# A convolution tile as three rounded products, and another pace for taps and norms in a two-block transformer kernel

## The chip, the core and the metric

The kernel runs on one core of a Trainium2 chip. The metric is the device time of one execution in microseconds; it is the time of the whole program, two layers of a first kind of block and then two layers of a second. Engines: PE (TensorE) multiplies matrices, DVE (VectorE), ACT (ScalarE) and POOL (GpSimd) work on tiles of 128 partitions, SP issues the weight DMAs. Each engine runs its own instructions in the order in which they are written, and waits on semaphores that the others raise.

## The reference, cut

Sequence 512, width 1024, float32. The change lies in the mixer of the first kind of block, which does attention with a window and a causal depthwise convolution of 31 taps side by side on one projection:

```python
u = _rms_norm(h, mix_norm[i])
q, k, v, ca, cg = jnp.split(u @ w_in[i], SPLITS, axis=-1)
q = _partial_rope(q.reshape(B, S, N_HEADS, HEAD_DIM), positions)
k = _partial_rope(k.reshape(B, S, N_KV_HEADS, HEAD_DIM), positions)
attn = _sliding_window_attention(q, k, v, sinks[i])
conv = _conformer_conv(ca, cg, conv_w[i], conv_b[i], conv_ln_g[i], conv_ln_b[i])
mixed = jnp.concatenate([_rms_norm(attn, attn_out_norm[i]),
                         _rms_norm(conv, conv_out_norm[i])], axis=-1)
h = h + mixed @ w_out[i]
...
def _conformer_conv(a, g, w_dw, b_dw, ln_g, ln_b):
    u = a * jax.nn.sigmoid(g)
    y = conv(u, w_dw) + b_dw        # 512 channels, each with 31 taps over time
    return jax.nn.silu(_layer_norm(y, ln_g, ln_b))
```

Around it stand two gated FFNs of 2816, a projection of a per-layer embedding (`p[i] @ w_ple[i]`, normed, "the embedding" below) and a gate. The second kind of block is not touched.

## The kernel before

**Layout and precision.** Activations lie transposed, features on partitions and 512 time steps along the free axis, in tiles of 128x512. A weight product in near full precision is three products of rounded operands (type fp32r): ACT rounds a 128x1024 weight tile (`act_split`, L328, raw to wh), DVE takes the remainder (`dve_split`, L332, wl), and PE does hi x hi, hi-weight x lo, lo-weight x hi (L346 to L348, or `pe_chunks`, L356 to L358). A "unit" is one such output tile: 8 chunks of 128 rows, 24 products. Weights stream by DMA from SP through four buffers. PE may start unit k when wl of k is there and the bank of unit k-2 has been read.

**The stage of the change** (`block1`) has three parts.

*Projections*, 14 units n = 0 to 13: convolution gate and value (n 0 to 7), keys (8), values (9), queries (10 to 13). In each, DVE reads the bank (L1106), takes the next weight remainder, multiplies gate and value into `upad` (odd n), later rotates keys and queries (`rotate`, L1061 to L1072) and does `TAPS_AFTER[n]` taps of the second channel tile (L1081, L1085, a running sum in PSUM). ACT rounds weights, does three tap products a unit (`act_tap`, L877 and L883, for channel tiles 0 and 2) and builds 31 diagonal matrices `diag` of the fourth tile's taps (L887). POOL adds ACT's products (L675); ACT may be three products ahead.

*Pairs*, m = 0 to 15, four heads' pairs for each of four query blocks. PE runs scores (L758, two pairs ahead), turn (L770, transposes of the probabilities) and values (L783); DVE `scale` (L1143) takes the scores and their maximum, ACT `exps` (L945) the exponentials, DVE `turn_back` (L1154) copies the turned probabilities. Between them stand: the 31 taps of the fourth channel tile on PE (L791, a diagonal matrix times a shifted input, in full float32), the rest of ACT's taps (five a pair) and DVE's, the layer norm's mean (L831, pair 6) and variance (L837, pair 8), its root on ACT (L965) and reciprocal and products on DVE (L1223, L1226, pair 10), the SiLU on ACT (L969, pair 11), eight embedding tiles on PE (L745 to L747, pairs 7 to 14) that DVE copies (L1130) and ACT squares (L931), and the output norm's statistic (L843, pair 13). `pe_fill` (L420) issues products whose result nobody reads: 4 at pair 5, 4 at pair 11, 6 behind the pairs.

*Tail*: attention norm (L1179) and output norm of the convolution (L1234, L1237), transposes of the attention output (L797), the embedding's statistic (L851), rounding to `fh` and `fl` (L983, L1242, L990, L1185), and the first two units of the output projection, whose convolution chunks (4 to 7) come before their attention chunks (0 to 3).

The order is written out by hand in the five engine functions.

## Time and profile before

| | us |
|---|---|
| median of 3 runs | 3876.05 |
| lowest, highest | 3874.99, 3879.52 |
| the profiled execution | 3877.19 |
| its span in the trace | 3875.4 |
| PE busy in the span | 3761.7 |
| DVE, ACT, POOL busy | 2353.7, 1511.6, 532.9 |
| mean granted clock of PE | 0.993 |

The profiled execution is a run of its own, so its time is not one of the three. Times in the timelines count from the start of the span. A count of PE rows counts records: a product in full float32 leaves two. "[1.90 <-ACT prob L945]" says that the engine stood idle for 1.90 us and that an instruction of ACT that wrote `prob` released it. A PE record lasts longer than its share of the array, since products overlap: the pace is the distance between starts. The granted clock is 1.00 at 2.4 GHz and 0.50 at 1.2 GHz.

### The profile page before, as it was taken

The numbers are of one execution on the slowest core, as the hardware profiler recorded it, in microseconds if no ns is written. First come the engines' busy times: TensorE is split into PE (matmuls) and PEld (weight loads), VectorE is DVE, ScalarE is ACT, GpSimd is POOL, SyncE is SP. The second block draws the span as 40 slices with busy tenths as digits, with TensorE's granted clock in tenths as the row PEclk, the third lists the DMA queues.
The fourth block names the chain that finished last, engine by engine and source line by source line (L and its number), as shares of the span: only waits on it lengthen the run. The fifth ranks groups of instructions, "written<-read, shape, count | busy, mean of one in ns | idle before, by whom it ended". The sixth has DMA issues, their size and how long they took to land.

```text
span 3875.4 us, 46681 instructions
## 1 busy us (share of the span) xinstructions
PE 3761.7 (97%) x17846; PEld 3061.1 (79%) x17846; DVE 2353.7 (61%) x3233; ACT 1511.6 (39%) x2191; POOL 532.9 (14%) x378
## 2 busy tenths in 40 slices
PE   8999989999999999999999999999999999999997
PEld 6888758888888885788887778788877878888886
DVE  5455766444644467744567685675568776675656
ACT  3223653222422265422243554343344454343333
POOL 1001641000100046100010023200010013220002
PEclk9999999999999999999999999999999999999999
DMA  4333203333333330233333100132233210023222
GB/s 151 97 98 105 81 17 93 98 98 100 105 97 95 97 109 22 68 98 98 97 107 103 56 28 1 39 98 94 97 105 120 66 39 7 12 87 98 95 96 82
DMA packets 87019, 315.01 MB, mean 81 GB/s; under 512 B 10016, under 2 KB 10400, under 8 KB 86176
## 3 DMA queue, kind: packets, MB, share of 16 engines
q1 hardware_dynamic: 83664, 302.43, 25.2%
q10 hardware_dynamic: 3152, 9.74, 0.8%
q8 instruction: 143, 2.34, 0.3%
q14 instruction: 60, 0.49, 0.0%
HBM read 307.94 MB, written 2.10 MB: 80 GB/s over the span
## 4 chain that ended last, share of the span: by engine, by line
PE 84%; DVE 10%; POOL 2%; ACT 2%; issue 2%; DMA 0%; DVEq 0%; POOLq 0%; ACTq 0%; SPq 0%
PE ps L346 20%; PE ps L348 20%; PE ps L347 20%; PE ps L356 4%; PE ps L358 3%; PE ps L357 3%; POOL y L675 1%; PE ps L2021 1%; DVE wl L332 1%; PE ps L1690 1%; PE ps L2040 1%; PE ps L1682 1%; PE ps L1847 1%; POOL rstd L390 1%; DVE tri L1657 1%
## 5 line engine op out<-in xcount | busy, mean ns | idle before, releaser
L328 ACT ACTIVATE wh<-raw 128x1024 fp32r<-128x1024 f32 x564 | 597.4, 1059 | 1595.1 <-PE ps L348 1312.4
L346 PE MATMUL ps<-xh,wh 128*128 128x512 f32 x2336 | 917.3, 393 | 11.5 <-DVE xl L411 10.9
L347 PE MATMUL ps<-xl,wh 128*128 128x512 f32 x2336 | 910.0, 390 | 0.0
L348 PE MATMUL ps<-xh,wl 128*128 128x512 f32 x2336 | 909.8, 389 | 0.0
L332 DVE TENSOR_TENSOR wl<-raw,wh 128x1024 fp32r<-128x1024 f32 x564 | 704.7, 1249 | 176.2 <-ACT wh L328 175.2
L346 PEld LDWEIGHTS ps<-xh,wh 128*128 128x128 f32 x2336 | 439.3, 188 | 107.9 <-issue 12.5
L347 PEld LDWEIGHTS ps<-xl,wh 128*128 128x128 f32 x2336 | 439.4, 188 | 93.9 <-issue 3.6
L348 PEld LDWEIGHTS ps<-xh,wl 128*128 128x128 f32 x2336 | 439.3, 188 | 91.7
L346 PE MATMUL ps<-fh,wh 128*128 128x512 f32 x1016 | 397.3, 391 | 4.0 <-DVE wl L332 4.0
L347 PE MATMUL ps<-fl,wh 128*128 128x512 f32 x1016 | 395.4, 389 | 0.0
L348 PE MATMUL ps<-fh,wl 128*128 128x512 f32 x1016 | 395.3, 389 | 0.0
L390 POOL TENSOR_TENSOR rstd<-rstd,sq 128x512 f32<-128x512 f32 x77 | 124.3, 1614 | 1649.8 <-ACT sq L385 1648.9
L508 DVE SCALAR_TENSOR_TENSOR h<-ps,h 128x512 f32<-128x512 f32 x144 | 99.5, 691 | 316.6 <-PE ps L348 245.2
L346 PEld LDWEIGHTS ps<-fh,wh 128*128 128x128 f32 x1016 | 190.7, 188 | 48.2 <-DVE wl L332 8.5
L348 PEld LDWEIGHTS ps<-fh,wl 128*128 128x128 f32 x1016 | 190.7, 188 | 39.7
L347 PEld LDWEIGHTS ps<-fl,wh 128*128 128x128 f32 x1016 | 190.7, 188 | 39.6 <-issue 0.5
L576 DVE TENSOR_TENSOR ubuf<-ps,rstd 128x512 f32<-128x512 f32 x88 | 60.8, 691 | 263.2 <-PE ps L348 263.2
L356 PE MATMUL ps<-xh,wh 128*128 128x512 f32 x448 | 194.8, 435 | 5.9 <-DVE wl L332 3.9
L675 POOL TENSOR_TENSOR y<-y,tap_out 128x512 f32<-128x512 f32 x120 | 171.7, 1431 | 81.2 <-ACT tap_out L883 73.7
L573 DVE TENSOR_TENSOR gbuf<-ps,rstd 128x512 f32<-128x512 f32 x88 | 60.8, 691 | 192.6 <-PE ps L348 192.5
L358 PE MATMUL ps<-xh,wl 128*128 128x512 f32 x448 | 176.3, 393 | 0.0
L357 PE MATMUL ps<-xl,wh 128*128 128x512 f32 x448 | 175.5, 392 | 0.0
(477 smaller groups left out, 5575.2 us busy)
## 6 DMA issues: line engine op xcount, KB each, us to landing
raw<-in_w SPq DMA_DIRECT2D x564, 512.0 KB, 3.5
con<-in_consts SPq DMA_DIRECT2D x1, 2053.5 KB, 14.1
h<-in_x SPq DMA_DIRECT2D x4, 512.0 KB, 7.1
p_t<-in_p ACTq DMA_DIRECT2D x4, 512.0 KB, 3.8
w1k<-in_w1c ACTq DMA_DIRECT2D x2, 1024.0 KB, 5.3
w1v<-in_w1c ACTq DMA_DIRECT2D x2, 1024.0 KB, 7.4
out<-h SPq DMA_DIRECT2D x8, 256.0 KB, 2.1
dup_k<-roped ACTq DMA_DIRECT2D x8, 128.0 KB, 3.5
```

The costliest lines, as they stand in the source:

```text
L328: nc.scalar.activation(wh[k % 2][:, :], raw[k % 4][:, :], ACT.Copy).then_inc(s["w_hi"], 1)
L332: nc.vector.tensor_tensor(wl[k % 2][:, :], raw[k % 4][:, :], wh[k % 2][:, :].bitcast(F32), ALU.subtract).then_inc(s["w_lo"], 1)
L346: nc.tensor.matmul(DB[k % 2][:, :], a, hi(q), start=(q == order[0]), stop=False)
L347: nc.tensor.matmul(DB[k % 2][:, :], a, lo(q), start=False, stop=False)
L348: last = nc.tensor.matmul(DB[k % 2][:, :], b, hi(q), start=False, stop=(q == order[-1]))
L356: nc.tensor.matmul(DB[k % 2][:, :], a, hi(q), start=start and n == 0, stop=False)
L357: nc.tensor.matmul(DB[k % 2][:, :], a, lo(q), start=False, stop=False)
L358: last = nc.tensor.matmul(DB[k % 2][:, :], b, hi(q), start=False, stop=stop and n == len(chunks) - 1)
L390: nc.gpsimd.tensor_tensor(acc[:, :], acc[:, :], sq[:, n % 2, :], ALU.add).then_inc(s["sq_add"], 1)
L508: nc.vector.scalar_tensor_tensor(h[:, j, :], DB[k % 2][:, :], factor, h[:, j, :], ALU.mult, ALU.add).then_inc(s["bank"], 1)
L573: v.tensor_tensor(gbuf[:, :], DB[k % 2][:, :], rstd[:, :], ALU.mult).then_inc(s["bank"], 1)
L675: nc.gpsimd.tensor_tensor(y[:, ct, :], y[:, ct, :], tap_out[:, i % 3, :], ALU.add)\
```

## The change

Four edits, all in `block1`, so twice in the program.

1. The fourth channel tile's 31 taps on PE are each three fp32r products: `diag_hi` x `up_hi`, `diag_hi` x `up_lo`, `diag_lo` x `up_hi`. ACT rounds the tile's taps (`tap_hi`) and its input (`up_hi`, 128x542); DVE takes both remainders and builds 31 matrices `diag_lo`. PE waits for `up_lo` before the first tap.
2. ACT's tap products: 45 in the projections and 4 behind them, then four a pair, instead of 36 and five a pair. DVE's taps of the second tile: four a pair instead of three.
3. Norms sooner: mean at pair 5, variance at 7, root and reciprocal at 8, SiLU at 9, embedding tiles at pairs 6 to 13, output statistic at 11, its root at 12 and its reciprocal at 13. Attention norms of three blocks and the second output weight's split at pair 14, and the roundings of the convolution in ACT's pair 14.
4. The fills are gone, and the tail's order on PE is: transposes of three blocks, last values, convolution chunks of unit 1, the embedding's statistic, half of the chunks of unit 0, last transposes, the other half, attention chunks.

```diff
+            PLE_AT = 6
+            SILU_AT = 9
+            TAPS_UNDER = (0, 0, 4, 3, 4, 3, 4, 3, 4, 4, 4, 4, 4, 4)
+            TAPS_AHEAD = 4
...
                     def tap(j):
                         pe.wait_ge(s["diag"], z("diag") + j + 1)
-                        mm(BK[4][:, :], diag[:, j, :], upad[:, PE_CT, j:j + T], start=(j == 0),
+                        mm(BK[4][:, :], diag_hi[:, j, :], up_hi[:, j:j + T], start=(j == 0), stop=False)
+                        mm(BK[4][:, :], diag_hi[:, j, :], up_lo[:, j:j + T], start=False, stop=False)
+                        mm(BK[4][:, :], diag_lo[:, j, :], up_hi[:, j:j + T], start=False,
                            stop=(j == TAPS - 1)).then_inc(s["tap"], 1)
...
-                        if m == 5:
-                            pe_fill(DB[0], 4)
                         turn(m)
...
-                        if m == 11:
-                            pe.wait_ge(s["o_ready"], z("o_ready") + 2)
-                            pe_fill(DB[0], 4)
...
-                    pe_fill(BK[2], 6)
...
+                    for i in range(done, done + TAPS_AHEAD):
+                        act_tap(act, s, st, i)
+                        done += 1
...
-                        for _ in range(5):
+                        for _ in range(4):
                             if done < N_PROD:
                                 act_tap(act, s, st, done)
...
+                        if m == 14:
+                            act_split(act, s, st, 0, o + U1_OUT + 1)
+                            for q in range(CT):
+                                act.wait_ge(s["conv_normed"], z("conv_normed") + q + 1)
+                                A(fh[:, 4 + q, :], y[:, q, :], ACT.Copy).then_inc(s["conv_hi"], 1)
...
+                        if n < 5:
+                            for j in range(7 * n, min(7 * n + 7, TAPS)):
+                                v.tensor_scalar(diag_lo[:, j, :], c("ident"), tap_lo[:, j:j + 1], None, ALU.mult)
+                        if n == 8:
+                            dve.wait_ge(s["gate"], z("gate") + 6)
+                            v.tensor_tensor(up_lo[:, :], upad[:, PE_CT, :], up_hi[:, :].bitcast(F32),
+                                            ALU.subtract).then_inc(s["conv_in"], 1)
...
+                        if m == 13:
+                            dve.wait_ge(s["cn_root"], z("cn_root") + 1)
+                            v.reciprocal(rstd[:, :], rstd[:, :]).then_inc(s["dve_step"], 1)
+                            dve.wait_ge(s["dve_step"], z("dve_step") + st.up("dve_step"))
+                            for q in range(CT):
+                                v.scalar_tensor_tensor(y[:, q, :], y[:, q, :], g("conv_out")[:, q:q + 1],
+                                                       rstd[:, :], ALU.mult, ALU.mult).then_inc(s["conv_normed"], 1)
+                        if m == 14:
+                            dve_split(dve, s, st, 0, o + U1_OUT + 1)
...
+                            for b in range(NB - 1):
+                                norm_o(b)
```

The order of ACT from the tap products of the last two projection units to those behind pair 1 and the exponentials next to them, before:

```order
L883 ACTIVATE tap_out<-upad,small_73 128x512 x4
L921 ACTIVATE p_hi<-p_t 128x1024
L328 ACTIVATE wh_59<-raw_57 128x1024
L945 ACT_TABLE_LOAD
L945 ACTIVATE prob,den<-sm,negm 128x128 x2
L883 ACTIVATE tap_out<-upad,small_73 128x512 x5
L945 ACTIVATE prob,den<-sm,negm 128x128 x2
L883 ACTIVATE tap_out<-upad,small_73 128x512 x5
L945 ACTIVATE prob,den<-sm,negm 128x128 x2
```

and with the change:

```order
L890 ACTIVATE tap_out<-upad,small_73 128x512 x8
L932 ACTIVATE p_hi<-p_t 128x1024
L328 ACTIVATE wh_59<-raw_57 128x1024
L890 ACTIVATE tap_out<-upad,small_73 128x512 x4
L959 ACT_TABLE_LOAD
L959 ACTIVATE prob,den<-sm,negm 128x128 x2
L890 ACTIVATE tap_out<-upad,small_73 128x512 x4
L959 ACTIVATE prob,den<-sm,negm 128x128 x2
L890 ACTIVATE tap_out<-upad,small_73 128x512 x4
```

The row of eight holds the four products of each of the last two units (before: one of unit 12 and the three of unit 13, the others in rows above). Four more stand behind the weight rounding, ahead of the first exponentials, and then four instead of five in each pair.

DVE in the ninth projection unit (n = 8), before:

```order
L1085 SCALAR_TENSOR_TENSOR ps<-upad,small_73,ps 128x512 x2
L1106 TENSOR_TENSOR gbuf<-ps,rstd 128x512
L332 TENSOR_TENSOR wl_60<-raw_56,wh_58 128x1024
L1085 SCALAR_TENSOR_TENSOR ps<-upad,small_73,ps 128x512 x4
L1106 TENSOR_TENSOR v_t<-ps,rstd 128x512
L332 TENSOR_TENSOR wl_61<-raw_57,wh_59 128x1024
```

and with the change:

```order
L1101 SCALAR_TENSOR_TENSOR ps<-upad,small_73,ps 128x512 x2
L1122 TENSOR_TENSOR gbuf<-ps,rstd 128x512
L332 TENSOR_TENSOR wl_60<-raw_56,wh_58 128x1024
L1141 TENSOR_TENSOR up_lo<-upad,up_hi 128x542
L1101 SCALAR_TENSOR_TENSOR ps<-upad,small_73,ps 128x512 x4
L1122 TENSOR_TENSOR v_t<-ps,rstd 128x512
L332 TENSOR_TENSOR wl_61<-raw_57,wh_59 128x1024
```

The remainder of the inputs stands ahead of the four taps.

DVE from the copy of the embedding in pair 13 (ple 5 of 0 to 7) to the last norm of the attention blocks, before:

```order
L1130 COPY e_t<-ps 128x512
L1154 COPY pt<-ps 128x512
L1130 COPY e_t<-ps 128x512
L1154 COPY pt<-ps 128x512
L1160 TENSOR_TENSOR es<-negm,small_73 128x8
L1130 COPY e_t<-ps 128x512
L1154 COPY pt<-ps 128x512
L1229 RECIPROCAL ss<-ss 128x3
L1179 SCALAR_TENSOR_TENSOR o_tok<-o_tok,ss,small_73 128x512 x3
L1234 RECIPROCAL rstd<-rstd 128x512
L1237 SCALAR_TENSOR_TENSOR y<-y,small_73,rstd 128x512 x4
```

and with the change, from pair 13 too (ple 6), to the turn of pair 15:

```order
L1158 COPY e_t<-ps 128x512
L1182 COPY pt<-ps 128x512
L1258 RECIPROCAL rstd<-rstd 128x512
L1261 SCALAR_TENSOR_TENSOR y<-y,small_73,rstd 128x512 x4
L1158 COPY e_t<-ps 128x512
L1182 COPY pt<-ps 128x512
L1188 TENSOR_TENSOR es<-negm,small_73 128x8
L332 TENSOR_TENSOR wl_61<-raw_55,wh_59 128x1024
L1266 RECIPROCAL ss<-ss 128x3
L1207 SCALAR_TENSOR_TENSOR o_tok<-o_tok,ss,small_73 128x512 x3
L1182 COPY pt<-ps 128x512
```

The reciprocal and the four products of the output norm now stand before the turns of pairs 14 and 15, and with them a weight remainder and three attention norms.

## Rows read from the trace of the kernel before

**Rows 1.** The page, its first part: busy time of each engine, share of the span, instructions.

```profile
PE 3761.7 (97%) x17846; PEld 3061.1 (79%) x17846; DVE 2353.7 (61%) x3233; ACT 1511.6 (39%) x2191; POOL 532.9 (14%) x378
```

**Rows 2.** Timeline of PE, 456 to 520: start, length, engine, line, operands, count, idle time before.

```profile
459.17 0.39 PE L347 MATMUL ps<-xl,wh 128*128 128x512 f32 x1
459.40 0.39 PE L348 MATMUL ps<-xh,wl 128*128 128x512 f32 x1
...
471.62 1.13 PE L758 MATMUL ps<-k_z,q_t 128*128 128x128 f32 x8 [0.56 <-DVE q_t L1072]
...
482.89 4.51 PE L791 MATMUL ps<-upad,diag 128*128 128x512 f32 x10
487.24 1.02 PE L758 MATMUL ps<-k_z,q_t 128*128 128x256 f32 x4
...
500.95 0.66 PE L770 MATMUL ps<-con,prob 128*128 128x128 f32 x4 [1.90 <-ACT prob L945]
...
511.47 3.67 PE L831 MATMUL ps<-y,con 128*128 128x512 f32 x8 [0.17 <-issue]
514.98 1.03 PE L758 MATMUL ps<-k_z,q_t 128*128 128x256 f32 x4
515.85 0.60 PE L770 MATMUL ps<-con,prob 128*128 128x128 f32 x4
516.28 1.00 PE L783 MATMUL ps<-v_tok,pt 128*128 128x64 f32 x8
517.09 0.48 PE L745 MATMUL ps<-p_hi,wh 128*128 128x512 f32 x1
```

**Rows 3.** Timeline of PE, 520 to 600, columns as above.

```profile
536.93 3.65 PE L420 MATMUL ps<-con 128*128 128x512 f32 x8
541.87 0.47 PE L745 MATMUL ps<-p_hi,wh 128*128 128x512 f32 x1 [1.28 <-DVE e_t L1130]
...
565.23 5.31 PE L420 MATMUL ps<-con 128*128 128x512 f32 x12
...
585.53 0.41 PE L346 MATMUL ps<-fh,wh 128*128 128x512 f32 x1
```

**Rows 4.** Timeline of POOL, 383 to 620: the additions of convolution taps.

```profile
457.43 8.74 POOL L675 TENSOR_TENSOR y<-y,tap_out 128x512 f32<-128x512 f32 x5 [1.42 <-ACT tap_out L883]
474.48 36.73 POOL L675 TENSOR_TENSOR y<-y,tap_out 128x512 f32<-128x512 f32 x26 [8.31 <-ACT tap_out L883]
```

**Rows 5.** Timeline of DVE, 383 to 600, beside an idle and a busy POOL.

```profile
421.83 1.23 DVE L332 TENSOR_TENSOR wl<-raw,wh 128x1024 fp32r<-128x1024 f32 x1 [0.33 <-ACT wh L328]
...
446.68 2.25 DVE L332 TENSOR_TENSOR wl<-raw,wh 128x1024 fp32r<-128x1024 f32 x1
...
461.61 1.76 DVE L1061 TENSOR_TENSOR fbuf<-gbuf,cos 128x512 f32<-128x512 f32 x1
...
466.36 0.68 DVE L1061 TENSOR_TENSOR fbuf<-ubuf,cos 128x512 f32<-128x512 f32 x1
...
533.60 3.34 DVE L1223 RECIPROCAL rstd<-rstd 128x512 f32<-128x512 f32 x1
536.97 3.34 DVE L1226 TENSOR_TENSOR y<-y,rstd 128x512 f32<-128x512 f32 x4
...
567.12 2.74 DVE L1237 SCALAR_TENSOR_TENSOR y<-y,small,rstd 128x512 f32<-128x512 f32 x4
```

**Rows 6.** Groups of DVE instructions by line: count, busy us and mean ns.

```profile
L550 DVE TENSOR_SCALAR turn<-turn 128x512 f32<-128x512 f32 x4 | 1.7, 429 | 0.1
```

**Rows 7.** Timeline of ACT, 383 to 595: the load of a function table.

```profile
554.40 1.28 ACT L977 ACT_TABLE_LOAD   x1
```

**Rows 8.** Timeline of PE in the second layer, 1498 to 1520.

```profile
1506.31 0.66 PE L770 MATMUL ps<-con,prob 128*128 128x128 f32 x4 [1.89 <-ACT prob L945]
...
1508.48 4.92 PE L420 MATMUL ps<-con 128*128 128x512 f32 x8
```

**Rows 9.** Two us there: length, busy PE, PEld, DVE, ACT, POOL, then PE's granted clock.

```profile
1508.00:1510.00 2.00, 2.00 (x4) 1.01 (x3) 1.93 (x6) 0.87 (x2) 1.84 (x3) 0.50 0.00 0
```

More of the change, by code:

```diff
@@ L845, in _, with conv_chunks @@
                             last.then_inc(s["cn_mm"], 1)
-                    values(PAIRS - 1)
                     for b in range(NB - 1):
                         out_tiles(b)
+                    values(PAIRS - 1)
+                    def conv_chunks(n, chunks):
+                        k = o + U1_OUT + n
+                        pe.wait_ge(s["w_lo"], k + 1)
+                        for q in chunks:
+                            pe.wait_ge(s["conv_lo"], z("conv_lo") + q - 3)
+                            pe_chunks(k, f_hi, f_lo, (q,), q == 4, False)
+                    conv_chunks(1, range(4, DC))
                     pe.wait_ge(s["e_add"], z("e_add") + DC - 1)
@@ L886, in act_diag @@
                 def act_diag(act, s, st, j):
[L887 removed]
+                    nc.scalar.activation(diag_hi[:, j, :], c("ident"), ACT.Copy,
                                          scale=taps[:, PE_CT, j:j + 1]).then_inc(s["diag"], 1)
@@ L907, in _ @@
                     done = built = 0
+                    A(tap_hi[:, :], taps[:, PE_CT, :], ACT.Copy).then_inc(s["gate"], 1)
                     for n in range(14):
@@ L913, in _ @@
                             A(sbuf[:, :], v_t[:, :], ACT.Sigmoid).then_inc(s["gate"], 1)
-                        for i in range(done, done + 3 if n >= 2 else done):
+                        if n == 8:
+                            act.wait_ge(s["conv_in"], z("conv_in") + CT)
+                            A(up_hi[:, :], upad[:, PE_CT, :], ACT.Copy).then_inc(s["gate"], 1)
+                        for i in range(done, done + TAPS_UNDER[n]):
                             act_tap(act, s, st, i)
```

105 lines of the change are left out of this document (50 added, 55 removed).

## The prediction

> **What bounds the kernel now.** I read the page first: PE is busy for 97% of the span [rows 1], so time is to be had only where PE idles, waits behind padding, or does work that could be cheaper. The edits touch one stretch, the mixer of the first block type, which runs twice. In the first layer it runs from the projections (from 384) to 585.5, where the third tile of the output projection starts [rows 3]. The timelines of the four engines over that stretch, in one clock, tell the rest. The reader is to see three parts.
>
> From about 446 to 471.6 PE waits for DVE: PE's scores of pair 0 start at 471.62, after a wait that a DVE instruction writing q_t ended [rows 2]. From 471.6 to 511.5 PE is nearly always busy, but its turn of pair 4 waits 1.90 us for ACT's exponentials [rows 2], and those queue behind ACT's tap products, which wait for POOL: POOL adds 26 taps in one run of 36.73 us, so 1.41 us each, until 511.2 [rows 4]. The mean of the layer norm needs the last of them, and PE starts it at 511.47 [rows 2]. So POOL sets the mean. From there to 585.53 (74.1 us) the chain goes to and fro between PE, DVE and ACT: 14 fill products pad PE's waits in a layer, two groups of 4 and one of 6 [rows 3]. I call the start of the scores S and the start of the mean M; before, M = S + 39.85.
>
> **Step 1, the taps of TensorE.** Five taps in full precision run from 482.89 to 487.24, 0.87 us a tap [rows 2]. The three products that replace each are of the form that the projections use, which start 0.23 us apart [rows 2]: 3 x 0.227 = 0.68 us. That is 0.19 us a tap, 31 taps, 5.9 us a layer, if PE bounds. The first 7 taps lie before S, where PE waits for DVE, and give nothing.
>
> **Step 2, S moves.** ACT now issues 49 tap products ahead of the first exponentials, not 36. POOL therefore has 47 additions, not 34, before S. Its idle gaps from 402 to 466 add up to about 11 us (10 gaps, the last of 1.42 us [rows 4]), and 13 additions of 1.36 us are 17.7 us. So POOL is busy without a break up to S and DVE works beside it. What this does to DVE is in the rows: the weight remainder takes 1.23 us beside an idle POOL and 2.25 beside a busy one; the rotation's product 0.68 against 1.76 [rows 5]. DVE has no slack left from the ninth projection tile on. On its chain to S the change puts:
> - the remainder of the rounded inputs (128x542, two operands from SBUF), 0.7 to 1.8 us; I take 1.3;
> - weight remainders of tiles 7, 8, 9 and 11 that now meet a busy POOL: 0.8 + 0.9 + 0.9 + 0.5 = 3.1 us;
> - the last two rotation products, at 466.4 and 469.3, now beside a busy POOL: 2 x 1.1 us and about 0.3 us on the sums behind them, 2.5 us.
> Together 6.9 us: S at 478.5 and not 471.6. The bounds: 0.7 us, if POOL cost nothing, and about 8.5. The 31 small products that build diag_lo (seven a tile) lie in the first five tiles; a 128x512 of that kind takes 0.43 us [rows 6], so at most 0.25 us each, 1.8 us a tile, about DVE's idle time there. I take nothing for them.
>
> No row shows this one-input operation beside a busy POOL. The Trainium skill, GPSIMD Engine Reference, Key points, says that GpSimd shares its SBUF interfaces with VectorE and that they contend when a VectorE instruction has two SBUF inputs or runs in a 2-port mode. For two inputs the trace agrees (0.68 against 1.76 us). By that rule the small products of tiles 2 to 4 would contend too, and the sum would grow towards rival C's; by the rows alone it stays.
>
> **Step 3, from S to M.** After S, PE's rows give each pair: scores 0.87, turn 0.43, values 0.8 [rows 2] (half of that for the first four pairs, which have one block of keys). Scores 0 and 1: 0.96. Pair 0: 5 taps 3.4 + 0.44 + 0.22 = 4.1. Pair 1: 4.5. Pairs 2 and 3: 4.9 each. Pair 4 with the last 4 taps: 4.45. Then scores, turn and values before the mean, which now stands behind pair 5: 2.2. The sum is 26.0. DVE's reading of the taps' bank, behind the end of the first query block, adds about 0.4. POOL has 13 additions left, 13 x 1.41 = 18.3 us after S, so it no longer sets M; ACT's exponentials, paced by four additions a pair (5.6 us against PE's 4.9), start two pairs ahead: those of pair 3 end at about 495.3, and PE's turn of it is due at 498.9. Against this, PE idles about 3.3 us before the last rotation and 3.8 before S, and the clock falls. Its price is in the second layer: after a wait of 1.89 us the stretch at 1508 shows a clock of 0.50, that is 1.2 and not 2.4 GHz, and eight fill records take 4.92 us [rows 8, 9] and not 3.65 [rows 3]. A longer dense stretch at that level costs somewhat more; I take 1.7. M = 478.5 + 26.4 + 1.7 = 506.6, that is 4.9 us sooner than 511.47.
>
> **Step 4, from M to the end.** I walked the chain with the durations of the rows, M as zero. One more pair stands behind the mean than before (10, not 9): 2.1 us of PE. Up to the variance nothing differs. The first reciprocal (3.34) with its four products (3.34) [rows 5] blocks DVE from 19.2 to 25.8, before PE had 3.65 us of fill and 1.28 of wait there [rows 3], now it waits 5.5. So these 4 fills buy nothing, and nor do the four behind pair 5: a wait takes their place. The output norm's statistics run at 38.2 to 41.7 and its root on ACT ends at 46.7. Each change between exponential and root costs ACT a table load of 1.28 [rows 7]: exponentials of pair 13 end at 49.0, PE turns at 49.2, DVE copies to 50.4, and only then come the second reciprocal and four products (3.34 + 2.74 [rows 5]) to 56.4. **That is the place that decides.** On DVE the last embedding copy, the turn of pair 14, a weight remainder and three attention norms are queued behind them; on ACT the weight rounding and four roundings of the convolution (some 5 us) stand ahead of the exponentials of pair 15, which end at 62.4. PE has nothing else and idles from 55.6 to 62.5. Before, the same norm ended at 58.4, but pairs 14 and 15 were done by then; now it ends at 56.4 with them open. Behind: turn and values 14 to 63.9, three transposes of the output to 65.7, values 15, four chunks (waiting once for DVE) to 70.1, the statistic 71.0, two chunks, transpose, two chunks to 74.3, and the eight attention chunks 5.5: 79.9. Before it was 74.1. So the stretch grows by 5.9 us although 12.2 us of fill left PE. On top the clock falls in the wait of 5.5 and in that of 7 us, both without fill now: 1.6 + 1.9 us.
>
> **The sum.** Per layer -4.9 + 5.9 + 3.5 = +4.5. In the second layer one such fall was there already (4.92 against 3.65), so +3.2. Together **+7.7 us**. The profiled execution took 3877.19 us (span 3875.4); it lies 1.1 us above the median of 3876.05, and I add the sum to the median: 3884 us. Nothing else in the program moves. A measurement of this kernel can tell about 0.2%, 7.75 us, from no change, so the forecast stands on that line.
>
> **Rivals.**
> A, the other side: **POOL does not slow DVE further**, because the additions fall where DVE reads PSUM. Then S = 472.3, M = 472.3 + 26.4 = 498.7, 12.8 us sooner. With the falls of the clock behind M (3.5) a layer gives -12.8 + 5.9 + 3.5 = -3.4, in all about -8: 3868. If the short waits also leave the clock up: -6.9 a layer, -15 in all, 3861. It decides at S: below about 475 the kernel is faster. For it: POOL still has slack in tiles 2 to 7, where fours and threes alternate. Against it: from tile 8 on there are four in every tile, and the rows of a busy POOL.
> B: **the clock does not fall** in the new waits, with S as forecast: -6.6 + 5.9 = -0.7 a layer, 3873, no change. Against it stands the fall after 1.89 us of wait [rows 8]; for it, that a like wait at 500.95 [rows 2] left the 4 fills behind it at 3.65 us.
> C: **the projections themselves stall**: four additions with the locks (1.36 x 4 + 1.6 = 7 us) are more than a tile's 5.44 us, ACT's tap products wait for POOL and the weight rounding behind them on ACT's queue comes late, and the small diagonal products each wait for an addition. Up to 6 us a layer more: 3896.
> D: the second norm's chain is shorter than walked (say the root is ready a pair earlier), 4 us a layer: 3876.
>
> **How the numbers follow.** Forecast 0.38, half of it beyond the line. A 0.22 (0.15 of it faster by over 0.2%), B and D 0.22, C 0.18. That gives faster 0.17, within 0.2% 0.42, slower 0.41. The range must reach to A with the clock kept and to C: 3861 to 3897.
>
> **What the profile would show.** S in the first layer at 478 (less than 474 for A, over 482 for C); the mean at 506; POOL's additions ended before 500; taps in triples 0.68 us apart; a PE wait of over 5 us for the embedding copy behind the reciprocal and one of over 6 before the turn of pair 15; a clock of 0.5 behind each; third tile of the output projection at about 590. The prediction is wrong if S does not move, or if the wait before pair 15 is under 3 us.

## The result and the profile after

The changed kernel takes 3882.59 us (median of 20 runs, 3881.07 to 3885.18), the kernel before 3877.41 us (20 runs beside it, 3874.99 to 3879.52). The ratio is 1.0014, with a 95% interval from 1.0008 to 1.002: 5.2 us slower, 0.14%. The forecast was 7.7 us slower. The profiled execution has a span of 3880.7 us (before 3875.4). Every experiment below is set against runs of the kernel before made beside it, whose medians lie between 3876.0 and 3877.6 us.

I read each trace by four points. All are counted from the first statistic product of the projections (before: 384.80 in the first layer, 1390.19 in the second). S is the start of the scores of pair 0, M that of the mean, T the last turn, E the third tile of the output projection.

| kernel, layer | S | M | T | E | M to E |
|---|---|---|---|---|---|
| before, 1 | 86.82 | 126.67 | 175.00 | 200.73 | 74.1 |
| before, 2 | 86.79 | 126.67 | 175.01 | 202.33 | 75.7 |
| after, 1 | 92.46 | 122.16 | 185.44 | 204.33 | 82.2 |
| after, 2 | 92.40 | 121.37 | 184.37 | 202.79 | 81.4 |

So the mean came 4.5 and 5.3 us sooner, and the stretch behind it grew by 8.1 and 5.8 us: +3.6 and +0.5 us. The rest of the 5.3 us of span lies outside: -0.4 us ahead of the first layer, and behind the second 2282.9 us before and 2284.5 after, where the diff changes nothing. Over all the kernels of this study that last stretch reads 2280.5 to 2285.8 us in the profiled executions, so 1.6 us there is no effect of the change.

TensorE's timeline of the changed kernel, first layer (start, length, engine, line, operands, count, idle time before and what ended it), answers to [rows 2, 3]:

```profile
476.89 2.05 PE L765 MATMUL ps<-k_z,q_t 128*128 128x128 f32 x8 [2.88 <-DVE q_t L1088]
478.59 0.77 PE L798 MATMUL ps<-up_hi,diag_hi 128*128 128x512 f32 x1
479.16 0.63 PE L799 MATMUL ps<-up_lo,diag_hi 128*128 128x512 f32 x1
479.59 0.63 PE L800 MATMUL ps<-up_hi,diag_lo 128*128 128x512 f32 x1
...
484.68 0.48 PE L798 MATMUL ps<-up_hi,diag_hi 128*128 128x512 f32 x1
485.00 0.39 PE L799 MATMUL ps<-up_lo,diag_hi 128*128 128x512 f32 x1
485.23 0.39 PE L800 MATMUL ps<-up_hi,diag_lo 128*128 128x512 f32 x1
...
488.25 0.60 PE L765 MATMUL ps<-k_z,q_t 128*128 128x128 f32 x4
...
506.59 3.67 PE L835 MATMUL ps<-y,con 128*128 128x512 f32 x8 [0.35 <-DVE y L1242]
...
532.98 0.80 PE L752 MATMUL ps<-p_hi,wh 128*128 128x512 f32 x1 [4.27 <-DVE e_t L1158]
...
557.12 0.66 PE L777 MATMUL ps<-con,prob 128*128 128x128 f32 x4 [2.54 <-ACT prob L959]
...
569.87 1.11 PE L777 MATMUL ps<-con,prob 128*128 128x128 f32 x4 [6.10 <-ACT prob L959]
570.78 1.80 PE L790 MATMUL ps<-v_tok,pt 128*128 128x64 f32 x8
...
588.76 0.41 PE L346 MATMUL ps<-fh,wh 128*128 128x512 f32 x1
```

Where fills stood before there are waits of 4.27 and 6.10 us now. Behind the waits of 2.88, 4.27 and 6.10 us the products start at about half their rate: the tap products 0.43 us apart, and 0.23 from 482.9 on. The windows view of these stretches shows the granted clock (the number behind POOL's) at 0.50, that is 1.2 GHz. It shows the same from 558 to 561, behind the wait of 2.54 us:

```profile
478.00:482.00 4.00, 4.00 (x13) 3.32 (x12) 1.26 (x8) 3.97 (x9) 3.78 (x3) 0.50 0.00 0
533.00:534.00 1.00, 1.00 (x3) 0.81 (x4) 0.52 (x1) 0.59 (x1) 0.27 (x1) 0.50 0.00 0
559.00:560.00 1.00, 1.00 (x4) 0.81 (x4) 1.00 (x1) 0.97 (x3) 0.61 (x1) 0.50 0.00 0
570.00:574.00 4.00, 4.00 (x20) 4.00 (x21) 2.67 (x6) 0.53 (x1) 0.00 (x0) 0.50 0.28 103
```

GpSimd's timeline (additions of taps, against [rows 4]) and DVE's (against [rows 5]) of the changed kernel:

```profile
414.14 41.42 POOL L682 TENSOR_TENSOR y<-y,tap_out 128x512 f32<-128x512 f32 x25 [2.90 <-ACT tap_out L890]
455.88 45.66 POOL L682 TENSOR_TENSOR y<-y,tap_out 128x512 f32<-128x512 f32 x29 [0.32 <-ACT tap_out L890]
```

```profile
396.02 1.46 DVE L1138 TENSOR_SCALAR diag_lo<-con,tap_lo 128x128 fp32r<-128x128 f32 x7
...
408.58 3.53 DVE L1138 TENSOR_SCALAR diag_lo<-con,tap_lo 128x128 fp32r<-128x128 f32 x7
...
429.49 1.51 DVE L332 TENSOR_TENSOR wl<-raw,wh 128x1024 fp32r<-128x1024 f32 x1 [2.67 <-ACT wh L328]
...
436.22 1.79 DVE L1141 TENSOR_TENSOR up_lo<-upad,up_hi 128x542 fp32r<-128x542 f32 x1
...
469.95 1.71 DVE L1077 TENSOR_TENSOR fbuf<-ubuf,cos 128x512 f32<-128x512 f32 x1
...
476.66 1.23 DVE L1160 TENSOR_SCALAR negsink<-small 128x8 f32<-128x8 f32 x1
```

From 414 to 501.5 GpSimd works without a break (one gap of 0.32 us). Seven of the small products for diag_lo take 1.46 us while it idles, and 3.53 beside it. The rotation's product that took 0.68 us [rows 5] takes 1.71. An operation on 128x8 takes 1.23 us; its like in the kernel before, at 471.39, took 0.16. From the wait of 2.67 us at 429.49, for ScalarE's rounding of the next weights, DVE has no further idle time up to S.

And the place before the last turn, on DVE, then on ScalarE:

```profile
558.42 3.34 DVE L1258 RECIPROCAL rstd<-rstd 128x512 f32<-128x512 f32 x1
561.80 2.74 DVE L1261 SCALAR_TENSOR_TENSOR y<-y,small,rstd 128x512 f32<-128x512 f32 x4
564.46 0.68 DVE L1158 COPY e_t<-ps 128x512 f32<-128x512 f32 x1
```

```profile
565.18 0.63 ACT L945 ACTIVATE tap_out<-e_t 128x512 f32<-128x512 f32 x1 [2.96 <-DVE e_t L1158]
565.71 1.04 ACT L328 ACTIVATE wh<-raw 128x1024 fp32r<-128x1024 f32 x1
566.66 2.17 ACT L1000 ACTIVATE fh<-y 128x512 fp32r<-128x512 f32 x4
568.74 0.49 ACT L959 ACTIVATE prob<-sm,negm 128x256 f32<-128x256 f32 x1
```

The last embedding copy stands behind the reciprocal and the four products. The square of it on ScalarE waits for the copy, and the roundings and the exponentials of pair 15 stand behind the square. This is the queue that the prediction described. Whether it sets the time is another question, and the experiments answer it.

### The profile page after: what moved, and what is told of

It reads as the page before. It is cut to its first block, busy times and chain, and to the rows that moved or that the text cites. A ratio compares the mean times of both kernels' runs of the same rounds, so it can differ in the third digit from the quotient of the medians.

```text
span 3880.7 us, 46769 instructions
## 1 busy us (share of the span) xinstructions
PE 3743.1 (96%) x17852; PEld 3074.3 (79%) x17852; DVE 2378.7 (61%) x3299; ACT 1519.5 (39%) x2199; POOL 545.0 (14%) x378
## 4 chain that ended last, share of the span: by engine, by line
PE 83%; DVE 9%; POOL 3%; ACT 2%; issue 2%; DMA 0%; DVEq 0%; POOLq 0%; ACTq 0%; SPq 0%
PE ps L346 20%; PE ps L348 20%; PE ps L347 20%; PE ps L356 4%; PE ps L358 4%; PE ps L357 3%; POOL y L682 2%; PE ps L2057 1%; PE ps L1726 1%; PE ps L1718 1%; PE ps L2076 1%; DVE wl L332 1%; PE ps L1883 1%; POOL rstd L390 1%; DVE tri L1693 1%
## 5 line engine op out<-in xcount | busy, mean ns | idle before, releaser
L682 POOL TENSOR_TENSOR y<-y,tap_out 128x512 f32<-128x512 f32 x120 | 184.6, 1539 | 49.9 <-ACT tap_out L890 41.0
```

Of the source, the lines that this page charges most:

```text
L682: nc.gpsimd.tensor_tensor(y[:, ct, :], y[:, ct, :], tap_out[:, i % 3, :], ALU.add)\
```

## The experiments

The rows of the table are first layer / second layer. "Against before" is the difference of the medians.

| kernel | S | M | M to E | us | against before | ratio, 95% interval |
|---|---|---|---|---|---|---|
| taps_only | 86.8 / 86.8 | 126.9 / 126.9 | 75.7 / 75.7 | 3877.43 | +1.1 | 1.0003 [0.9994, 1.0012] |
| full_taps | 90.2 / 90.1 | 121.0 / 120.9 | 82.8 / 82.0 | 3882.28 | +5.9 | 1.0014 [1.0005, 1.0023] |
| fills_back | 92.4 / 92.4 | 121.4 / 122.2 | 78.1 / 79.5 | 3877.27 | +0.9 | 1.0001 [0.9992, 1.001] |
| shifted | 92.5 / 92.5 | 122.1 / 123.0 | 80.7 / 82.3 | 3880.7 | +4.4 | 1.0009 [1.0, 1.0018] |
| shifted_late | 92.5 / 92.5 | 121.5 / 122.9 | 79.2 / 79.6 | 3875.57 | -1.0 | 0.9994 [0.9985, 1.0003] |
| early_stat | 86.8 / 86.8 | 126.7 / 126.7 | 80.0 / 78.8 | 3886.08 | +9.5 | 1.0022 [1.0013, 1.0031] |
| norm_behind | 92.5 / 92.4 | 122.9 / 122.9 | 83.6 / 83.3 | 3882.48 | +4.8 | 1.0015 [1.0006, 1.0024] |
| more_ahead | 92.6 / 92.5 | 119.0 / 120.7 | 82.3 / 81.9 | 3879.69 | +3.1 | 1.0005 [0.9996, 1.0014] |
| late_more | 92.5 / 92.5 | 121.2 / 119.8 | 79.2 / 79.1 | 3870.7 | -5.3 | 0.9984 [0.9975, 0.9993] |
| late_more_light | 95.5 / 95.5 | 124.4 / 125.7 | 79.2 / 77.5 | 3880.55 | +4.5 | 1.001 [1.0001, 1.0019] |
| late_full | 90.1 / 90.2 | 117.5 / 117.5 | 77.6 / 79.2 | 3865.76 | -10.3 | 0.9971 [0.996, 0.9982] |

**The taps alone.** The kernel before with the new tap() and what it needs on ScalarE and DVE, and no other edit.

```diff
-                        mm(BK[4][:, :], diag[:, j, :], upad[:, PE_CT, j:j + T], start=(j == 0),
+                        mm(BK[4][:, :], diag_hi[:, j, :], up_hi[:, j:j + T], start=(j == 0), stop=False)
+                        mm(BK[4][:, :], diag_hi[:, j, :], up_lo[:, j:j + T], start=False, stop=False)
+                        mm(BK[4][:, :], diag_lo[:, j, :], up_hi[:, j:j + T], start=False,
```

> The kernel before with the cheaper taps alone (three rounded products for each of the 31 taps of TensorE's convolution tile, with the remainders that they need); pacing, norms and tail stay as they were. My theory: GpSimd sets the start of the mean (511.5 us in the first layer), so a PE that saves 0.19 us a tap gains nothing there. The start of pair 0's scores comes 1 to 2 us later (the remainder of the inputs, 31 small products on DVE), which GpSimd's run absorbs. Time: within 2 us of the kernel before. Rival 'PE bounds': 31 x 0.19 us = 5.9 us a layer less, 11.6 us faster than before.

S and M stand where they stood before (86.8 and 126.9). So 31 cheaper taps give nothing while GpSimd sets the mean, as expected. DVE's remainders cost nothing either while GpSimd still pauses: even the 1 to 2 us later S that was expected did not come.

**The changed kernel without the new taps.**

```diff
-                        mm(BK[4][:, :], diag_hi[:, j, :], up_hi[:, j:j + T], start=(j == 0), stop=False)
...
+                        mm(BK[4][:, :], diag_hi[:, j, :], upad[:, PE_CT, j:j + T], start=(j == 0),
```

> The changed kernel with its pacing, norms and tail, but the taps in full precision again (one product of 0.87 us instead of three of 0.23), and so without the remainders of taps and inputs. My theory: the start of pair 0's scores comes about 1.5 to 2 us sooner than in the changed kernel (475 instead of 476.9), because DVE loses the input remainder and the small products; between there and the mean PE pays 24 x 0.19 = 4.6 us more, so the mean starts about 3 us later (509.5 instead of 506.6). Time: about 5 us over the changed kernel. Rival 'the small products on DVE cost more than the taps save': not slower than the changed kernel.

The time is that of the changed kernel (+5.9 against +5.2 us over before, with intervals of about 3.5 and 2.3 us on either side), so my forecast of 5 us on top of it fell and the rival held. S is 2.3 us sooner, and M is not later but 1.2 and 0.4 us sooner. The rows of this kernel's TensorE beside those of the changed one tell why:

```profile
474.56 1.13 PE L760 MATMUL ps<-k_z,q_t 128*128 128x128 f32 x8 [2.22 <-DVE q_t L1077]
475.52 4.46 PE L793 MATMUL ps<-upad,diag_hi 128*128 128x512 f32 x10
```

A tap in full precision takes 0.86 us (the next scores start 4.30 us behind the start of the five). Five taps of three products take 3.57 us (484.68 to 488.25 above), 0.71 a tap: the products stand 0.23 to 0.24 us apart, and the first of a group, behind another operation, takes 0.32. The 24 taps behind S save 24 x 0.15 = 3.6 us. But in the changed kernel the clock is down from the wait of 2.88 us before S on: its scores take 1.70 us to the next product and not 0.96, and the ten tap products behind them 4.35 us and not 2.41, some 2.7 us in all. Behind the wait of 2.22 us here the scores and taps run at full rate. So 3.6 - 2.7 = 0.9 us should be won between S and M. The table has 1.1 us in the first layer and 1.8 in the second, where 2.3 were lost ahead of S.

**GpSimd beside DVE.** The changed kernel with half-width additions on GpSimd (the other half of the sums is left out).

```diff
-                        nc.gpsimd.tensor_tensor(y[:, ct, :], y[:, ct, :], tap_out[:, i % 3, :], ALU.add)\
+                        nc.gpsimd.tensor_tensor(y[:, ct, 0:256], y[:, ct, 0:256], tap_out[:, i % 3, 0:256], ALU.add)\
```

> The changed kernel with GpSimd's additions of the tap products on half of the columns (the other half of the sums is left out), so that GpSimd is busy about half as long and idles between. Theory (GpSimd beside it slows DVE's operations that read SBUF): the start of pair 0's scores moves from 92.4 us behind the start of the projections back to 87 to 88.5; the small products of seven for diag_lo take 1.5 us and not 2.5 to 3.5 a tile, the rotation's products 0.7 and not 1.7. Rival (it is the added work and its order on DVE and ScalarE, whoever runs beside it): the scores start at 91 or later.

S comes at 85.0 and 84.4 us, sooner than expected and even sooner than in the kernel before (86.8), with all of the added work on DVE and ScalarE in place. GpSimd and DVE in this kernel:

```profile
412.33 3.25 POOL L682 TENSOR_TENSOR y<-y,tap_out 128x256 f32<-128x256 f32 x4 [2.89 <-ACT tap_out L890]
```

```profile
433.95 0.72 DVE L1141 TENSOR_TENSOR up_lo<-upad,up_hi 128x542 fp32r<-128x542 f32 x1
...
459.27 1.23 DVE L1077 TENSOR_TENSOR fbuf<-gbuf,cos 128x512 f32<-128x512 f32 x1
...
467.12 0.69 DVE L1077 TENSOR_TENSOR fbuf<-gbuf,cos 128x512 f32<-128x512 f32 x1
...
469.67 0.69 DVE L1160 TENSOR_SCALAR negsink<-small 128x8 f32<-128x8 f32 x1
```

Up to 457.5 GpSimd now pauses for 1.3 to 2.9 us between its groups, and the remainder of the inputs takes 0.72 us (1.79 in the changed kernel), the last rotation product 0.69 (0.99). So what moved S is GpSimd's work, not the list of work on the other engines. In the first layer S comes 7.5 us sooner (92.46 to 84.99), and the two traces show how they divide. From the remainder of the inputs to S, DVE has the same operations in both kernels and no wait in either: 40.7 us in the changed kernel (436.22 to 476.89) and 36.0 here (433.95 to 469.90). So 4.7 us are DVE's operations taking longer. The other 2.8 us are there already at the remainder, and nearly all of them are the wait of 2.67 us for ScalarE's rounding, behind tap products that wait for GpSimd; here that wait is 0.40 us. One execution only was timed (3863.17 us), which is of use only for where it was won: M came 10 us sooner.

**The fills.** The changed kernel with five padding products before the embedding product of pair 9 and seven before the turn of pair 15.

```diff
+                        if m == 15:
+                            pe.wait_ge(s["max_ready"], z("max_ready") + 30)
+                            pe_fill(BK[0], 7)
                         turn(m)
...
+                        if m == 9:
+                            pe.wait_ge(s["o_ready"], z("o_ready") + 2)
+                            pe_fill(DB[0], 5)
```

> The changed kernel with two groups of padding products back on TensorE: 5 before the turn of pair 9, once the third part of the output is ready, and 7 before the turn of pair 15. My theory: the half clock behind the waits of 4.3 and 6.1 us goes, 1.6 to 2 us each, so the time falls by about 3 us a layer, 5 to 6 us in all. Rival: padding of this length ends before the wait does, the clock falls all the same or the padding itself delays the turns, and the time is that of the changed kernel within 2 us.

As expected in kind, a little less in size: the time goes back to that of the kernel before (+0.9 where the changed kernel had +5.2), and M to E is 4.1 and 2.0 us shorter. Its TensorE, first layer:

```profile
528.23 4.51 PE L420 MATMUL ps<-con 128*128 128x512 f32 x10
...
561.61 6.23 PE L420 MATMUL ps<-con 128*128 128x512 f32 x14
...
569.28 1.48 PE L806 MATMUL ps<-con,o_tok 128*128 128x128 f32 x12
```

The waits are still there, but filled. Behind them the twelve transposes take 1.48 us, in the changed kernel they had taken 2.77 at half clock. Nothing else differs, so filling the waits takes away most of the loss, and the rows put it down to the clock; why the waits are there is another question. The single runs spread from 3872.1 to 3881.4 us, wider than before's; the clock still falls behind shorter waits in one run and not in another.

**Which sooner step costs.** First the kernel before with cheaper taps, pacing and all norms one pair sooner, but with its old tail (second reciprocal behind the last pair) and ten of its fourteen fills. Against the changed kernel the first reciprocal, the SiLU, the output norm's statistic and its root stand one pair later, too.

```diff
-            PLE_AT = 7
+            PLE_AT = 6
...
-                        if m == 13:
+                        if m == 12:
                             for q in range(CT):
                                 pe.wait_ge(s["conv_sq"], z("conv_sq") + q + 1)
```

> The kernel before with the cheaper taps, the new pacing and the first norm, the embedding part and the output statistic one pair sooner, but with the tail as it was: the second reciprocal and its products after the last pair, output tiles and output products in the old order, padding kept except behind pair 5. My theory: the mean starts at 506.6 us as in the changed kernel, and from there to the third output tile it takes 74.1 + 2.1 = 76.2 us, not 82.2. That is 2.8 us a layer sooner than before: about 5.6 us faster than the kernel before. Rival 'the place of the second norm does not matter': the stretch behind the mean is about 82 us here too, and the time is that of the changed kernel.

The rival held: M stands at 122 as forecast, but M to E is 80.7 and 82.3 us, not 76.2. The block that I had named, the reciprocal and its products ahead of the last turns, is not in this kernel, and the loss is. So something else costs it. Two steps are left that were sooner here too: the output norm's statistic on TensorE, 3.4 us, which now stands ahead of the last scores, and its root on ScalarE with two table loads, which stands ahead of the last two exponentials. Three runs tested this new theory. With both put back in 'shifted':

```diff
-                        if m == 12:
+                        if m == 13:
                             for q in range(CT):
                                 pe.wait_ge(s["conv_sq"], z("conv_sq") + q + 1)
...
-                        if m == 13:
+                        if m == 14:
                             act.wait_ge(s["cn_mm"], z("cn_mm") + 1)
```

> The kernel 'shifted' with one thing put back: the output norm's statistic on TensorE stands behind pair 13 again (not 12) and its root on ScalarE behind pair 14 (not 13). New theory: the statistic (3.4 us of TensorE) in front of the last scores, and the root with its two table loads in front of the last two exponentials, is what cost 'shifted' and the changed kernel their gain behind the mean. Then the stretch from the mean to the third output tile is 74.1 + 2.1 = 76.2 us here (shifted: 80.7), with the mean at 122.1 us after the start of the projections as in 'shifted' and 126.7 in the kernel before: 2.4 us a layer less than before, about 3872. Rival, my first theory (it is the reciprocal and products on DVE that are in the way, or another consequence of the sooner mean): no change against 'shifted', about 3881.

Against before it goes from +4.4 to -1.0 us (3875.6, where about 3872 was expected). M to E falls by 1.5 and 2.7 us to 79.2 and 79.6, not to 76.2: the last turn still waits 2.09 us for the exponentials behind the root, where before it waited 0.64, and a part of the 3 us that are missing I did not trace. The other way round, the kernel before with nothing but this moved one pair ahead:

```diff
-                        if m == 13:
+                        if m == 12:
                             for q in range(CT):
                                 pe.wait_ge(s["conv_sq"], z("conv_sq") + q + 1)
...
-                        if m == 14:
+                        if m == 13:
                             act.wait_ge(s["cn_mm"], z("cn_mm") + 1)
```

> The kernel before with one thing moved: the output norm's statistic on TensorE behind pair 12 (not 13), its root and that of the first three attention norms on ScalarE behind pair 13 (not 14). GpSimd's squares that the statistic reads are ready by then (544.2 us, the statistic would start near 549). New theory: the last turn comes 4.6 us later and the third output tile about 4.5 us, 9 us in all: about 3885. Rival: the place costs nothing, since TensorE idles or pads there anyway: within 2 us of the kernel before, or 1 to 2 us faster.

3886.08 us, 9.5 us over the kernel before. Moving work that TensorE and ScalarE have to do anyway by one pair costs more than the whole change did. Its TensorE:

```profile
548.41 1.88 PE L843 MATMUL ps<-sq,con 128*128 128x512 f32 x4
...
559.71 1.11 PE L770 MATMUL ps<-con,prob 128*128 128x128 f32 x4 [3.60 <-ACT prob L945]
```

The turn of pair 14 waits 3.60 us for the exponentials and then runs at half clock (1.11 us, in [rows 2] 0.60). So a part of the 9.5 us is a fall of the clock again. ScalarE's root in this kernel, and then in the kernel before:

```profile
556.38 0.69 ACT L977 ACTIVATE rstd<-ps,con 128x512 f32<-128x512 f32 x1
```

```profile
556.47 0.69 ACT L977 ACTIVATE rstd<-ps,con 128x512 f32<-128x512 f32 x1 [0.78 <-PE ps L843]
```

The root comes no sooner by its sooner place (171.7 us behind the start of the projections in both), but the exponentials of pair 14 now stand behind it. Statistic and root were moved together, so which of the two costs more stays open. Last, the changed kernel with only my block moved, reciprocal, products and roundings behind pair 15:

```diff
-                        if m == 13:
+                        if m == 15:
                             dve.wait_ge(s["cn_root"], z("cn_root") + 1)
                             v.reciprocal(rstd[:, :], rstd[:, :]).then_inc(s["dve_step"], 1)
```

> The changed kernel with the second reciprocal, its four products (DVE) and the four roundings of the convolution (ScalarE) behind pair 15 and not behind pairs 13 and 14; statistic, root and the new tail stay where the change put them. The prediction's theory (this block, standing ahead of turns 14 and 15, is the place that decides): TensorE's wait of 6.1 us before the last turn falls below 1 us, the last turn stands at about 57 us behind the mean and not at 63, but the norm then ends at about 64 to 65 and the convolution's chunks wait for it, so the third output tile gains 2 us a layer: about 4 us faster than the changed kernel, 3878 to 3879. Rival (the statistic and root, which stay, make all of the cost): the wait shrinks but the third output tile comes no sooner, 3882 to 3883.

The rival held. TensorE's rows:

```profile
565.08 0.66 PE L777 MATMUL ps<-con,prob 128*128 128x128 f32 x4 [1.28 <-ACT prob L959]
566.60 1.98 PE L806 MATMUL ps<-con,o_tok 128*128 128x128 f32 x12
575.25 0.77 PE L356 MATMUL ps<-fh,wh 128*128 128x512 f32 x1 [5.62 <-DVE fl L1274]
```

The wait before the last turn falls from 6.10 to 1.28 us, and 5.62 us of it come back before the first chunk of the convolution, which needs the same norm. E comes no sooner (+4.8 against +5.2 us over before). The longest wait of the stretch was a place where the loss showed, not its cause. The changed kernel with nothing but statistic and root put back was not run, so how much of its own 5.2 us is their place, and how much the clock in unfilled waits, is not shown: putting them back was worth 5.4 us in 'shifted', filling the waits 4.3 us here, and the two overlap, since the wait of 3.58 us behind the root in 'shifted' also ends at half clock (its turn takes 1.11 us).

**More taps in the waits.** Thirteen of the 31 taps before S and not seven, first in the changed kernel, then in 'shifted_late'.

```diff
-                    for j in range(3):
+                    for j in range(5):
                         tap(j)
                     rotate(4)
-                    for j in range(3, 7):
+                    for j in range(5, 13):
                         tap(j)
```

> The changed kernel with 13 of TensorE's 31 taps before pair 0's scores and not 7 (5 before the last rotation, 8 behind it, 18 left to the pairs). In the changed kernel TensorE idles 1.7 us before the last rotation and 2.9 us before the scores, and runs at half clock for 5 us behind. Theory: the six taps (4.2 us) fill these waits, the clock stays, so the scores start where they did (92.4 us after the start of the projections, or 0.5 later) and the mean starts 4 to 6 us sooner (116 to 118 instead of 121.4 to 122.2), until GpSimd's last addition (117.1) bounds it. The gain is 4 us a layer, 8 in all against the changed kernel: about 3874. Rival: ScalarE's exponentials, paced by four tap products a pair, or GpSimd bound the pairs, and the mean moves by less than 1.5 us.

> The kernel 'shifted_late' (pacing, first norm a pair sooner, old places of the output norm's statistic and root, old tail) with 13 of TensorE's taps before pair 0's scores and not 7, as in 'more_ahead'. If both gains add up: the mean at 119 to 120.7 us after the start of the projections (shifted_late: 121.4 and 122.9), the rest as there, so 2.3 us a layer sooner: about 3871, faster than the kernel before by 5 to 6 us. Rival: the exponentials, paced by GpSimd, give it back behind the mean: 3875.

In the changed kernel M comes 3.2 and 0.7 us sooner with S in place, and the time is 2 us less (+3.1 against +5.2). That is a quarter of what I expected, and the intervals of the two kernels overlap. The wait before S is gone, but one before the turn of pair 3, for exponentials that GpSimd paces, takes part of the gain (1.91 us, and 3.17 in 'late_more'; the changed kernel has none there in its first layer and 1.79 us in its second). 'late_more' came out as forecast, 3870.7 us, faster than the kernel before by 5.3 us; its M moved by 0.3 and 3.1 us.

**A lighter pace for GpSimd.** 'late_more' with 45 tap products ahead of the scores and not 49.

```diff
-            TAPS_UNDER = (0, 0, 4, 3, 4, 3, 4, 3, 4, 4, 4, 4, 4, 4)
-            TAPS_AHEAD = 4
+            TAPS_UNDER = (0, 0, 4, 4, 4, 4, 4, 4, 4, 3, 3, 3, 3, 3)
+            TAPS_AHEAD = 2
```

> 'late_more' with fewer tap products ahead of the scores: 45 and not 49 (four under each of seven projection tiles, then three, 2 behind the last), so that GpSimd pauses in the last five tiles, where DVE has the rotation on its way to the scores. Theory (GpSimd beside it slows DVE): pair 0's scores start at 89 to 91 us behind the start of the projections and not at 92.5. GpSimd's last addition comes 2 to 4 us later than the 117.1 of the changed kernel, so the mean starts at 119 to 121 and the time is 3868 to 3872. Rival: GpSimd's queue never empties (its additions take longer than their share of a tile), the scores stay at 92 and the exponentials wait longer: as 'late_more' or slower.

A miss: S comes 3 us later, not 2 us sooner, and the time rises by 10 us. Its DVE and TensorE, first layer:

```profile
432.92 1.51 DVE L332 TENSOR_TENSOR wl<-raw,wh 128x1024 fp32r<-128x1024 f32 x1 [2.66 <-ACT wh L328]
```

```profile
428.13 0.50 PE L346 MATMUL ps<-xh,wh 128*128 128x512 f32 x1 [0.92 <-DVE wl L332]
434.49 0.50 PE L346 MATMUL ps<-xh,wh 128*128 128x512 f32 x1 [0.60 <-DVE wl L332]
```

ScalarE's rounding of the next weights stands behind tap products that wait for GpSimd, DVE waits for the rounding, and the projections themselves stall (three waits of 0.5 to 0.9 us at tile starts; the changed kernel has none there before 450). This is the prediction's rival C. Three tap products more in the early tiles were enough to bring it about. The changed kernel stands right at that edge: its DVE has one such wait, 2.67 us at 429.49. No projection tile of TensorE is late by it, but S is, since DVE has no idle time left behind it.

**All that paid, without the new taps.** 'shifted_late' with taps in full precision, eleven of them ahead of S.

```diff
-            diag_hi = f("diag_hi", [P, TAPS, P], F32R)
-            diag_lo = Layout(nc, e_at, 16384)("diag_lo", [P, TAPS, P], F32R)
+            diag_hi = f("diag_hi", [P, TAPS, P])
...
-                    for j in range(3, 7):
+                    for j in range(5, 11):
                         tap(j)
```

> 'shifted_late' with TensorE's taps in full precision again (0.86 us each) and 11 of them before pair 0's scores. Theory: without the remainders on DVE the scores start at 90.2 to 90.7 us behind the start of the projections (shifted_late 92.5), the pairs carry 20 x 0.16 = 3.2 us more of TensorE than with rounded taps, and the mean starts at 118 to 120: the rounded taps are worth nothing, this kernel is at 3868 to 3873, level with or below 'late_more'. Rival (the rounded taps pay once TensorE bounds): slower than 'late_more' by 3 us or more.

3865.76 us (7 runs, 3864.41 to 3866.42), 10.3 us faster than the kernel before, 2 us below what was expected, and the fastest of the kernels that compute the whole result. S and M in its first layer:

```profile
474.80 1.13 PE L760 MATMUL ps<-k_z,q_t 128*128 128x128 f32 x8 [0.49 <-DVE q_t L1075]
...
502.19 3.67 PE L831 MATMUL ps<-y,con 128*128 128x512 f32 x8 [0.35 <-DVE y L1217]
```

The dearer taps fill the waits ahead of S down to 0.49 us, S is 2.4 us sooner without the remainders, and M stands at 117.5 in both layers, 2.3 to 3.7 us sooner than in 'late_more'. So the pacing, the first norm's sooner place and taps in the waits are worth 10 us together. 'late_more' has the same with the three products (and two taps more ahead) and is 5 us behind (ten of its eleven times lie above all seven of this kernel, though the two intervals against before touch): in these surroundings the rounded taps do not pay, and seem to cost about 5 us.

## Why the prediction was right or wrong

- **Bound before.** Right: GpSimd set the mean. 'taps_only' moved neither S nor M.
- **Step 1**, the size of a tap. Mis-sized: 0.15 us saved a tap, not 0.19 (0.86 against 0.71 us; the products stand 0.23 to 0.24 us apart and not 0.227, and the first of a group adds 0.09 us). Its use was misjudged more: of 3.6 us between S and M, 1.1 were left in the first layer and 1.8 in the second.
- **Step 2**, S moves by 6.9 us. Measured 5.6. The cause, GpSimd's work, is shown by 'half_adds', and so is the way: mostly DVE's operations beside it, as forecast, and 2.7 us of waiting for ScalarE's rounding, which the walk did not have on this chain. By 'full_taps' the pacing makes 3.3 us of it (forecast 5.6) and the remainders of taps and inputs 2.3 (forecast 1.3), which alone ('taps_only') cost nothing. The assumption that the small products for diag_lo take nothing held for the first two tiles only. The rule of the Trainium skill (GPSIMD Engine Reference, Key points), that a VectorE operation in a 2-port mode contends too, agrees with the rows: 1.46 us for seven beside an idle GpSimd, 2.50 and 3.53 beside a busy one. That these products run in such a mode no row shows. Its other result, rival C, came at this pace only as DVE's one wait; TensorE's tiles stalled in 'late_more_light'.
- **Step 3**, M at 506.6 us. Measured 506.59, but that is luck, by errors that cancel: S came at 476.89 and not 478.5 (5.6 against 6.9 us later than before, and the stage itself started 0.4 us sooner in this execution), and from S to M it took 29.7 us, not 28.1, since the clock's fall before S cost 2.7 us and not 1.7 and a tap 0.71 and not 0.68.
- **Step 4**, +5.9 us and 3.5 us of clock. Measured 8.1 in the first layer against 9.4, and 5.8 in the second against 8.1 (the fall that was there before counted off). The waits came where the walk put them: 4.27 us (forecast 5.5) for the embedding copy and 6.10 (7) before the turn of pair 15, with a clock of 0.50 behind each. But **"the place that decides"** was the wrong step. Moving that block away ('norm_behind') gained nothing, and leaving it out of the edit ('shifted', which differs in more than that) saved 0.8 us, within the noise. What the walk gave a line and no weight, the output norm's statistic and its root ahead of the last scores and exponentials, costs 9.5 us by itself when the kernel before is given it one pair sooner. How the changed kernel's own 5.2 us divide between that place and the clock is not shown. That fills can be dropped where a wait takes their place, "these 4 fills buy nothing", was wrong by itself: the fall of the clock that I priced separately is just what they bought, and twelve fills, placed in the two long waits, brought 4.3 us.
- **The sum**, +7.7 us. Measured +5.2. Ahead of M they gained 4.5 and 5.3 us (forecast 4.9). Behind M the two layers grew by 1.3 and 2.3 us less than forecast; 1.2 us of the profiled difference lie outside them.
- **Rivals.** A did not come: S moved later. B did not: the clock is at 0.50 in four places. D did not: the waits are there. C is real, but one step further on; its small products did not each wait for an addition, since seven of them lost 1.0 and 2.1 us and not seven times that.
- The two tests that the prediction named, S that does not move and a wait under 3 us before pair 15, both spoke for it. Of its other signs two missed: GpSimd's additions ended at 501.5 and not before 500, and the wait for the embedding copy was 4.27 us and not over 5. The tests could not tell a right chain from a wrong one: the 6 us wait was there and yet did not set the time.

## What to carry to other kernels

A long wait shows where a loss becomes visible; before it is called the cause, move the work that ends it and see whether the wait only moves too. When steps are pulled ahead in a loop of three engines, price each by what stands behind it on its queue at the new place: a statistic and a root that went one pair ahead of the last scores and exponentials cost 9.5 us where the work itself did not change. An engine kept busy without a break can cost the one beside it more than it gains (S came 3.3 us later by GpSimd's pace alone), and the spare time of a waiting TensorE is better filled with work that is due later (taps) than emptied.

## What the runs showed of the hardware

- One-input operations of DVE slow down beside GpSimd as two-input ones do: seven products of 128x128 take 1.46, 2.50 or 3.53 us, and one of 128x8 takes 1.23 us in the changed kernel, where the kernel before has, on DVE's timeline:

```profile
471.39 0.16 DVE L1132 TENSOR_SCALAR negsink<-small 128x8 f32<-128x8 f32 x1
```

- The smallest operation loses 1.07 us by it, one of 128x512 the same 1.08 (0.68 to 1.76). Beside additions of half the width ('half_adds') the same two take 0.69 and 1.23 us: they lose 0.53 and 0.55, half as much. So it reads like a wait for the addition under way to end, not like a lower rate. Not every operation pays the full price: the last rotation product lost 0.31 us (0.99) in the changed kernel and nothing (0.69) in 'half_adds', both beside a busy GpSimd, as a wait for the rest of an addition would have it. Products that read a bank of PSUM and one tile of SBUF (L1122, L1080) take 0.69 us beside a busy GpSimd as beside an idle one.
- TensorE's granted clock stood at 0.50, 1.2 of 2.4 GHz, behind waits of 2.54, 2.88, 4.27 and 6.10 us, and behind shorter waits it falls in one layer and not in the other of the same code: from the last transposes of the output (574.49 in the first layer) to the third tile the kernel before takes 11.04 us in its first layer, at a clock of 1.00, and 12.63 in its second, at 0.86. Behind a wait of 2.14 us at 577.23 the clock is 1.00 there, behind one of 2.15 us at 1582.63 it is 0.53. Some 1.6 us a layer can come or go by that alone, so a difference under 2 us between two profiled executions says little.
